# A gated-delta layer step: one TensorE transposition for two heads, decay factors scaled and first inverses made on GpSimd

## What is computed

```
kk = jnp.einsum('bnhid,bnhjd->bnhij', k, k)
a_mat = jnp.where(strict, beta[..., None] * kk * decay, 0.0) + jnp.eye(L, dtype=f32)
rhs = jnp.concatenate([v * beta[..., None], k * (beta * jnp.exp(gc))[..., None]], axis=-1)
sol = lax.linalg.triangular_solve(a_mat, rhs, left_side=True, lower=True, unit_diagonal=True)
...
qk = jnp.einsum('bnhid,bnhjd->bnhij', q, k) * decay
...
def step(s, inp):
    v_new = u_c - jnp.einsum('bhld,bhde->bhle', w_c, s)
    o = jnp.einsum('bhld,bhde->bhle', qd_c, s) + jnp.einsum('bhij,bhje->bhie', qk_c, v_new)
    s = s * gl_c[..., None, None] + jnp.einsum('bhld,bhle->bhde', kd_c, v_new)
```

## Time and profile before

| | us |
|---|---|
| median of 3 runs | 2017.8 |
| the profiled execution, its own time | 2012.97 |
| span of its trace | 2011.3 |
| group 0 of the delta stage, from its first pair products | 779.3 to 821.75 |
| group 1 | 821.75 to 862.05 |
| group 2 | 862.05 to 904.98 |
| group 3 | 904.98 to 945.69 |
| group 4 and its scan | 945.69 to 985.5 |

### The profile page before, as it was taken

The page is one execution under the profiler, slowest core; times in us unless marked ns, Lnnn a source line. Parts: engine busy times, 40 slices in busy tenths (PEclk is TensorE's granted clock), DMA queues, the critical chain, the costliest instruction groups (busy, mean ns, idle before and its releaser), DMA issues.

```text
span 2011.3 us, 34281 instructions
## 1 busy us (share of the span) xinstructions
PE 1936.1 (96%) x14050; PEld 1762.1 (88%) x14050; DVE 756.9 (38%) x1498; ACT 630.4 (31%) x1267; POOL 589.8 (29%) x456
## 2 busy tenths in 40 slices
PE   7999999999998998899799999999999999999998
PEld 7899999999995676678699879999999999999996
DVE  5211677111126764556643190222222222222225
ACT  5101222100016774344443244222222222222222
POOL 3111111111123003634264144333333333333333
PEclk9999999999999998999899999999999999999999
DMA  4322222622218213311253232111111111111114
GB/s 120 102 90 91 80 90 92 238 89 89 89 58 274 98 65 86 96 55 29 64 175 117 81 133 81 42 43 43 42 42 43 42 42 43 43 42 42 42 64 167
DMA packets 159274, 169.22 MB, mean 84 GB/s; under 512 B 14187, under 2 KB 130043, under 8 KB 159150
## 3 DMA queue, kind: packets, MB, share of 16 engines
q1 hardware_dynamic: 152814, 141.52, 22.6%
q10 hardware_dynamic: 6336, 25.96, 3.2%
HBM read 126.84 MB, written 40.55 MB: 83 GB/s over the span
## 4 chain that ended last, share of the span: by engine, by line
PE 49%; DVE 1%; ACT 0%; POOL 0%; issue 0%; DVEq 0%
PE t_B L2509 20%; PE t_B L2496 19%; PE t_B L2441 5%; PE t_B L2473 4%; DVE t_y L2356 1%; PE t_B L2451 0%; DVE t_y L2347 0%; DVE t_act_lo L2316 0%; ACT t_act_hi L2169 0%; DVE t_y L2386 0%; POOL t_wm_lo L2086 0%; ACT t_act_hi L2167 0%; DVE t_acc L2403 0%; DVE t_acc L2380 0%; DVE t_merged_lo L2363 0%
## 5 line engine op out<-in xcount | busy, mean ns | idle before, releaser
L2403 DVE TENSOR_TENSOR t_acc<-t_acc,t_B 128x512 f32<-128x512 f32 x252 | 173.3, 688 | 538.5 <-PE t_B L2509 538.5
L116 PE MATMUL i_ps<-x_hi,i_w_lo 128*128 128x384 f32 x1008 | 336.8, 334 | 0.0
L116 PE MATMUL i_ps<-x_hi,i_w_hi 128*128 128x384 f32 x1008 | 336.7, 334 | 0.0
L116 PE MATMUL i_ps<-x_lo,i_w_hi 128*128 128x384 f32 x1008 | 336.7, 334 | 0.0
L2496 PE MATMUL t_B<-t_merged_hi,t_wm_lo 128*128 128x384 f32 x768 | 256.9, 335 | 1.0 <-POOL t_wm_lo L2086 1.0
L2496 PE MATMUL t_B<-t_merged_lo,t_wm_hi 128*128 128x384 f32 x768 | 256.6, 334 | 0.0
L2496 PE MATMUL t_B<-t_merged_hi,t_wm_hi 128*128 128x384 f32 x768 | 256.6, 334 | 0.0
L106 POOL TENSOR_TENSOR i_w_lo<-i_w_raw,i_w_hi 128x1024 fp32r<-128x1024 f32 x44 | 105.7, 2403 | 432.2 <-ACT i_w_hi L101 432.2
L2086 POOL TENSOR_TENSOR t_wm_lo<-t_raw,t_wm_hi 128x1024 fp32r<-128x1024 f32 x49 | 119.0, 2428 | 295.9 <-ACT t_wm_hi L2161 295.9
L116 PEld LDWEIGHTS i_ps<-x_hi,i_w_lo 128*128 128x128 f32 x1008 | 189.2, 188 | 0.0
L116 PEld LDWEIGHTS i_ps<-x_lo,i_w_hi 128*128 128x128 f32 x1008 | 189.3, 188 | 0.0
(11 more groups left out here) (357 smaller groups left out, 3480.7 us busy)
## 6 DMA issues: line engine op xcount, KB each, us to landing
proj<-i_out ACTq DMA_DIRECT2D x44, 576.0 KB, 2.8
i_w_raw<-in_w_in SPq DMA_DIRECT2D x44, 512.0 KB, 3.7
t_raw<-in_w_up SPq DMA_DIRECT2D x32, 512.0 KB, 4.1
t_raw<-in_w_down SPq DMA_DIRECT2D x32, 512.0 KB, 3.5
t_gates<-proj SPq DMA_DIRECT2D x48, 192.0 KB, 2.6
a_k_cache<-in_cache_attn_k SPq DMA_DIRECT2D x8, 1024.0 KB, 8.0
a_v_cache<-in_cache_attn_v SPq DMA_DIRECT2D x8, 1024.0 KB, 5.4
d_c<-proj SPq DMA_DIRECT2D x3, 1536.0 KB, 7.6
```

The source lines that it names most:

```text
L116: last = pe.matmul(out, a[s][:, c, :], b[:, c, tokens], start=k == 0, stop=k == n - 1)
L2403: dve.tensor_tensor(a, a, B[(ND * j + d) % 4][:, :], ALU.add).then_inc(added, 1)
```

## The change

What it does:

- The channels of a group lie as [partition, chunk, channel block, token]. So two heads of one chunk are 128 adjacent columns, and "turn" takes four `pe.transpose` per chunk, each for two heads, where it took eight products. The loads now go chunk by chunk: 4 DMAs of 128 x 12 rows of 64 tokens (256 B), where one had rows of 256 tokens (1024 B), and `c0` takes 4 DMAs with such rows, where 2 had rows of 128 tokens (512 B).
- GpSimd multiplies `E` by `s_` for a whole group ("cols" has a part on GpSimd, one 128x512 operation), and "pair" on VectorE waits for that. `kd` takes `ers`, the product of `er` and `s_`.
- Step "x0" goes: its products on PE, two VectorE operations per chunk (1604), and `S0` on GpSimd (1412, step "turn"). In their place GpSimd makes `DD[1]` as identity minus the first masked block, in step "pair", after a wait for its own masking. "x0t" turns `DD[1]` into `DD[0]`.
- "sums" and "cols" of group g + 1 stand at other places: for g = 0 in steps "3a" and "3b", with the squares on ScalarE; else in "4b" and "5b". Before, "sums" stood after "solve", and "cols" after "pair" of the next group.
- `STEPS` keeps an empty step "turned" where "x0" stood, so scan items keep their step.

The diff's core (the rest gives waits and indices their new numbers and shapes; `head_c(n, c)` is the block c of chunk n, `landed(g)` is 16 for each load of the groups in this buffer up to g):

```diff
@@ -1117,10 +1117,10 @@
...
     def steps(n):
-        return (["pair", "turn", "x0", "x0t"] + [f"{j}{x}" for j in range(1, levels(n)) for x in "ab"]
+        return (["pair", "turn", "x0t"] + [f"{j}{x}" for j in range(1, levels(n)) for x in "ab"]
...

-    STEPS = ["pair", "turn", "x0", "x0t"] + [f"{j}{x}" for j in range(1, len(LEVELS)) for x in "ab"] + ["solve"]
+    STEPS = ["pair", "turn", "turned", "x0t"] + [f"{j}{x}" for j in range(1, len(LEVELS)) for x in "ab"] + ["solve"]
@@ -1150,14 +1150,14 @@
...
         if g:
-            out["pair"].insert(0, ("grp", g, "cols"))
...
             out["2b"].append(("grp", g + 1, "decay"))
-            out["solve"].append(("grp", g + 1, "sums"))
+            out["4b" if g else "3a"].insert(0, ("grp", g + 1, "sums"))
+            out["5b" if g else "3b"].append(("grp", g + 1, "cols"))
@@ -1178,9 +1178,9 @@
...
         if kind == "grp":
-            return {"decay": ("pool", "pe", "act"), "sums": ("pool" if n else "act", "pe", "dve"), "cols": ("pe", "act", "dve")}[s].count(eng)
+            return {"decay": ("pool", "pe", "act"), "sums": ("pool" if n > 1 else "act", "pe", "dve"), "cols": ("pe", "act", "dve", "pool")}[s].count(eng)
         if kind == "prep":
-            return {"pair": ("pe", "dve", "pool"), "turn": ("pe", "act", "dve", "pool"), "x0": ("pe", "dve"),
+            return {"pair": ("pe", "dve", "pool"), "turn": ("pe", "act", "dve"),
@@ -1314,10 +1319,10 @@
...
             def conv(g):
-                ts = first_token(GROUPS[g][0])
-                w = L * len(GROUPS[g])
-                sp.dma_start(C[g % 2][:, :, 0:w], env.proj[3 * AW:3 * AW + CONV, ts:ts + w].rearrange(
-                    "(c p) t -> p c t", p=P)).then_inc(c_in[g % 2], 16)
+                for n in GROUPS[g]:
+                    ts = first_token(n)
+                    sp.dma_start(C[g % 2][:, slot(n), :, :], env.proj[3 * AW:3 * AW + CONV, ts:ts + L].rearrange(
+                        "(c p) t -> p c t", p=P)).then_inc(c_in[g % 2], 16)
@@ -1361,12 +1366,20 @@
...
                 if kind == "grp" and s == "sums":
-                    w = L * len(GROUPS[n])
-                    pool.wait_ge(c_in[n % 2], 16 * ((n + 1) // 2))
+                    m = len(GROUPS[n])
+                    pool.wait_ge(c_in[n % 2], landed(n))
...
                     for i in range(2):
-                        half_c = C[n % 2][:, 4 * i:4 * i + 4, 0:w]
-                        pool.tensor_tensor(sq[i][:, :, 0:w], half_c, half_c, ALU.mult).then_inc(sq_made, 1)
+                        half_c = C[n % 2][:, 0:m, 4 * i:4 * i + 4, :].rearrange("p m h t -> p m (h t)")
+                        pool.tensor_tensor(sq[i][:, 0:m, :, :].rearrange("p m h t -> p m (h t)"), half_c, half_c,
+                                           ALU.mult).then_inc(sq_made, 1)
+                    continue
+                if kind == "grp" and s == "cols":
+                    m = GROUPS[n]
+                    wait(pool, "act", "grp", n, "decay")
+                    wait(pool, "dve", *item)
+                    e = E[n % 2][:, 0:len(m), :, :]
+                    did("pool", pool.tensor_tensor(e, e, bc(s_[:, m[0]:m[-1] + 1, :], 3, L), ALU.mult), item)
@@ -1392,7 +1405,12 @@
...
                     K = KQ[k][:, :, 1, :]
-                    ins = pool.tensor_tensor(M[k][:, 0:2, :, :], bc(K, 1, 2), bc(env.levc[:, 0:2, :], 2, 2), ALU.mult)
+                    pool.tensor_tensor(M[k][:, 0:2, :, :], bc(K, 1, 2), bc(env.levc[:, 0:2, :], 2, 2), ALU.mult
+                                       ).then_inc(first_blocks, 1)
+                    if n >= 4:
+                        wait(pool, "pe", "prep", solved(n - 4), "solve")
+                    pool.wait_ge(first_blocks, n + 1)
+                    ins = pool.tensor_tensor(DD[k][:, 1, :, :], bc(env.identc[:, :], 1, 2), M[k][:, 0, :, :], ALU.subtract)
@@ -1462,9 +1474,15 @@
...
                     elif s == "sums":
-                        act.wait_ge(env.c_in, 32)
+                        if n == 0:
+                            act.wait_ge(env.c_in, 64)
+                        else:
+                            act.wait_ge(c_in[1], landed(1))
+                            wait(act, "pe", "grp", 0, "sums")
                         for i in range(2):
-                            act.activation(sq[i][:, :, 0:w], C[0][:, 4 * i:4 * i + 4, 0:w], ACT.Square).then_inc(sq_made, 1)
+                            act.activation(sq[i][:, :, :, :].rearrange("p m h t -> p m (h t)"),
+                                           C[n][:, :, 4 * i:4 * i + 4, :].rearrange("p m h t -> p m (h t)"), ACT.Square
+                                           ).then_inc(sq_made, 1)
@@ -1573,12 +1591,14 @@
...
                         step(dve.tensor_tensor(s_[:, tiles, :], r2[:, tiles, :], beta[:, tiles, :], ALU.mult))
-                        ins = dve.tensor_scalar(negs[:, tiles, :], s_[:, tiles, :], -1.0, None, ALU.mult)
+                        if n == 0:
+                            dve.wait_ge(gexp, 3)
+                        ins = dve.tensor_tensor(ers[:, tiles, :], er[:, tiles, :], s_[:, tiles, :], ALU.mult)
...
                     if s == "pair":
-                        wait(dve, "act", "grp", n // 4, "decay")
+                        wait(dve, "pool", "grp", n // 4, "cols")
@@ -1589,26 +1609,15 @@
...
                             wait(dve, "pe", "heads", 3, "write")
-                        if n == 0:
-                            dve.wait_ge(gexp, 3)
...
                         dve.tensor_tensor(kbe[k][:, :, :], pairs(B[k][:, 0:256]), bc(eg[:, n, :], 2, P), ALU.mult)
-                        ins = dve.tensor_tensor(kd[n % 8][:, :, :], pairs(B[k][:, 0:256]), bc(er[:, n, :], 2, P), ALU.mult)
-                    elif s == "x0":
-                        wait(dve, "dve", "grp", n // 4, "cols")
-                        wait(dve, "pool", "prep", n, "turn")
-                        if n >= 4:
-                            wait(dve, "pe", "prep", n - 4, f"{last_level(n - 4)}a")
-                        for p in range(2):
-                            ins = dve.scalar_tensor_tensor(out=DD[k][:, 0, p, :], in0=B[k][:, p * L:p * L + L],
-                                                           scalar=negs[:, n, p:p + 1], in1=S0[k][:, p, :],
-                                                           op0=ALU.mult, op1=ALU.add)
+                        ins = dve.tensor_tensor(kd[n % 8][:, :, :], pairs(B[k][:, 0:256]), bc(ers[:, n, :], 2, P), ALU.mult)
...
                             wait(dve, "act", "prep", n, "x0t")
-                            wait(dve, "dve", "prep", n, "x0")
+                            wait(dve, "pool", "prep", n, "pair")
@@ -1726,32 +1735,27 @@
...
                         if n == 0:
-                            pe.wait_ge(env.c_in, 32)
+                            pe.wait_ge(env.c_in, 64)
                         elif n % 4 == 0:
-                            pe.wait_ge(c_in[n // 4 % 2], 16 * ((n // 4 + 1) // 2))
+                            pe.wait_ge(c_in[n // 4 % 2], landed(n // 4))
...
                             h = 2 * p + x
-                            ins = pe.matmul(b[half(x), 2 * L * p:2 * L * p + 2 * L], Cn[:, 4 + h, tok(n)], Cn[:, h:h + 5:4, tok(n)],
+                            ins = pe.matmul(b[half(x), 2 * L * p:2 * L * p + 2 * L], head_c(n, 4 + h), Cn[:, k, h:h + 5:4, :],
...
                         for i in range(2):
-                            for x, p in XP:
+                            for p in range(2):
                                 a = (2 * i + p) * P
-                                ins = pe.matmul(b[half(x), a:a + P], Cn[:, 4 + 4 * i + 2 * p + x, tok(n)], env.ident[:, :],
-                                                start=True, stop=True)
-                    elif s == "x0":
+                                ins = pe.transpose(b[:, a:a + P], Cn[:, k, 4 + 4 * i + 2 * p:6 + 4 * i + 2 * p, :].rearrange("p x t -> p (x t)"),
+                                                   env.ident[:, :])
+                    elif s == "x0t":
                         wait(pe, "dve", "prep", n, "turn")
-                        wait(pe, "pool", "prep", n, "turn")
+                        wait(pe, "pool", "prep", n, "pair")
                         for x, p in XP:
-                            ins = pe.matmul(b[half(x), p * L:p * L + L], M[k][half(x), 0, p, :], S0[k][half(x), p, :],
-                                            start=True, stop=True)
-                    elif s == "x0t":
-                        wait(pe, "dve", "prep", n, "x0")
-                        for x, p in XP:
-                            ins = pe.matmul(b[half(x), P + p * L:P + p * L + L], DD[k][half(x), 0, p, :],
+                            ins = pe.matmul(b[half(x), p * L:p * L + L], DD[k][half(x), 1, p, :],
...
```

37 lines of the change are left out of this document (17 added, 20 removed).

## The result

The changed kernel took 2035.7 us (median of 5 executions, 2031.5 to 2039.4), the kernel before 2018.8 beside it. The ratio is 1.0085, 95% interval 1.0068 to 1.0102: slower, by 17 us where +11.2 was predicted.

| part | before | after | difference | predicted |
|---|---|---|---|---|
| up to the first pair products | 779.31 | 785.38 | +6.1 | +0.5 |
| group 0 | 42.4 | 50.2 | +7.8 | +5.0 |
| group 1 | 40.3 | 44.1 | +3.8 | +1.7 |
| group 2 | 42.9 | 46.9 | +4.0 | +3.65 |
| group 3 | 40.7 | 44.1 | +3.4 | -0.2 |

A forecast was written before the change was run, and what follows sets the result against it. PE, nearly back to back, was taken to set the delta stage's pace, with group 0's mask chain lacking slack. Group terms of +9.15, attention +0.5 and clock +1.6 gave +11.2 on 2017.8: 2029.0 us, range 2014 to 2041.

The forecast's parts named there:

- Start of groups 2 and 3, -2.0: Heads of groups 2 and 3: second read and all behind it sooner with x0 gone, -2.0 us, bounds -1.3 and -2.25.
- Group 0, +5.0: Group 0: squares, table load and scaling ahead of the masks make them 6.9 us late; +5.0 us, bounds +3.5 and +6.5.
- Ends of groups 1 to 3, +1.7, +3.65, -0.2: Group ends: sums await squares and a load +3.0 us later, the norm follows, columns await Z7; net us per group.
- Short rows cost as much as those twice as long: Rival on the loads: 256 B rows cost 30 ns a packet like 512 B ones; 2037 us, chance 0.10.
- Group 4, -1.0: Last group, with two chunks: a sooner start makes it 1.0 us shorter.
- Attention, +0.5: c0's smaller packets ahead of the caches, while PE works on earlier blocks: +0.5 us, bounds 0 and 5.8.
- The clock, one fall, +1.6: PE's new waits at four places: one fall to 1.2 GHz counted in full, +1.6 us, bounds 0 and 6.4.
- The clock falls at all the heads: Rival: four clock falls at 1.6 us instead of one, perhaps because transpositions don't count as busy; 2033.8 us, chance 0.10.
- PE's stream decides: Rival on the delta stage: new waits fall into slack and the saved 12.4 us return in full; 2005.4 us, chance 0.14.

The follow-up runs named there:

- e2: The changed kernel with each chunk's four transpositions issued twice over into the same places: 2030.5 us, 1.0076 of the kernel before.
- e3: The changed kernel with x0t's products and copies one step earlier, ahead of the first out and second read: 2030.3 us, 1.0080 of the kernel before.
- e7: The changed kernel with c0's four transfers issued behind all the caches of attention: 2028.8 us, 1.0066 of the kernel before.
- e1: The changed kernel with each chunk turned by eight products with the identity, not four transpositions: 2036.8 us, 1.0091 of the kernel before.
- e4: The kernel before with only the new layout, loads with rows of 256 B and c0 in four transfers: 2018.1 us, ratio 1.0012.
- e5: The changed kernel with group 1's sums and columns back behind 4b and 5b: 2025.7 us, 1.0048 of the kernel before.
- e6: The changed kernel with the sums of groups 2 to 4 behind the norm, not ahead: 2029.8 us, 1.0057 of the kernel before.
- e9: e8 with c0's four transfers behind the caches of attention: 2007.5 us, 0.9964 of the kernel before.
- e12: e9 with idle products filling PE's waits ahead of group 0's first and second writes of the streams' states: 2009.3 us, 0.9957 of the kernel before.
- e8: The changed kernel's operations reordered (sums, columns, scaling, x0t moved; half the squares of groups 2 to 4 on ScalarE): 2011.3 us, 0.9973 of the kernel before.

## Why the prediction was right, and where its sizes were off

*Sign, main term and mechanism* were right: an order that puts new work ahead of the masks and the norm, and the squares on the path, costs more than the shorter stream gives. With the order mended, the same operations beat the kernel before.

*Start of groups 2 and 3, -2.0.* x0t came 9.7 us behind the pair products, 9.3 forecast and 11.5 before. The forecast gap of 2.9 us was 2.3; that gaps cost the clock as well stood in a rival.

*Group 0, +5.0.* The masks were 6.4 late (6.9 forecast); moving sums and columns back gave 7.5 us by the ratios and 9.2 in the profile. In e2 and e3 (clocks 0.88 and 0.89, against 0.81) the group was 5.4 to 5.9 longer than before, so the chain was sized well; the other 2 us in the profiled execution, which put it above the bound of +6.5, are most likely clock.

*Ends of groups 1 to 3, +1.7, +3.65, -0.2.* At a full clock group 1 took 40.5 (e7) and group 2 45.4 (e1, whose turn is longer), which is +0.2 and +2.5; group 3 took 40.2 at a full clock, though with e3's order, which is -0.5. So these terms were too high, by 1.5, 1.2 and 0.3 us. The price of 20 ns a packet was right, but I added all of the packets' growth to the load, and it was 1.6 us longer and not 3.0. The other mis-sized part is the norm: I took 1.7 to 2.0 us for it, and behind the squares it took 1.23, since 1.65 was its length beside them. In group 2 `turn0` thus came 36.2 us behind the pair products, against 34.9 before: +1.3 and not +3.0. "Short rows cost as much as those twice as long" is refuted in this case: 20.6 ns a packet of 256 B, 30 of 512. The Trainium skill (DMA: Bandwidth & Descriptors, Specifications) asks for at least 512 B a transfer for the full rate. The rate did fall, to 12.4 GB/s an engine from 17 at 512 B and 20 at 1024, by an estimate from these times; that a row of 256 B costs no less than one of 512, as the prediction read it, did not hold.

*Group 4, -1.0:* -1.3.

*Attention, +0.5: too low.* I reasoned that PE works on earlier blocks meanwhile. The rows show all caches behind c0 late, and the stage with them: 3.1 to 3.9 us more with four transfers than with two (under e7). The ratio of e4, +2.4 with 2.7 of uncertainty, agrees. It was inside my bounds, and the earlier trace rows pointed the other way: where the 16 engines are busy throughout, a longer transfer has no slack in which to hide. The other 2.7 us of the 6.1 in the table lie ahead of c0's issue and behind the stage's start, where profiles differ by as much whatever the kernel; the profile of the kernel before is itself 4.8 us faster than the median.

*The clock, one fall, +1.6: the step that failed in size.* 41 us at half speed instead of 7. The same code but for c0 (changed kernel and e7) had stages of 223.2 and 214.6 us at 41 and 17 us of low clock: 8.6 us for 24. By that the 34 us more than before are worth some 12 us in the profiled execution, in the medians less, since the profiles of the changed kernel and of e1, e2, e3, e5, e6 and e7 have 17 to 41, 27 on average: (27 - 7) x 0.36 = 7 us. The price of 0.36 comes from two profiles, but the lists of executions bear it out: in the four sets of the kernel before, 0.001 of mean clock, which is 4 us at the low level, went with 1.0 to 1.5 us, so 0.25 to 0.37 us each. I had said that "most of the lost time falls where PE then waits anyway"; the pair products of group 1 at 3.68 us in place of 1.97 (e9, e12) speak against it. "The clock falls at all the heads" was nearer to what happened than my forecast. Its named reason, the transposition, was wrong (e1, e2). What brings the falls is the order: with the same operations in e8's order the mean clock over all executions was 0.9880 and not 0.9806. That it does so through the waits is likely and rests on one execution of e12.

*"PE's stream decides":* refuted by e2, where 8 us of added work cost nothing.

So of +17 us in the medians, about 7.5 are the order in group 0 (its falls included), 3 to 4 c0, and about 1 the other groups apart from falls of the clock (+0.2, +2.5, -0.5, and -1.3 in group 4); the rest, some 5, is put down to those falls. That the order costs it is shown: e8 is 23 us faster with the same operations. The single shares are not measured that well; by the ratios each carries some 5 us, and only the profiles part them. That the sum of 11.2 lies as near to 17 as it does is in part luck: terms too high by 3 us at the ends of the groups made up for part of the clock and of c0.

## What to carry to other kernels

When a change makes an engine's stream shorter, look for what it waited with: here some 12 us of saved products turned into gaps, and several were followed by 3 to 10 us at half the clock. Before placing a new step in an in-order queue, write down what stands behind it on each of its engines; work that nobody awaits soon (here a scaling due 20 us later) belongs behind the chain, not ahead. A transfer placed ahead of others in a queue that is full delays all of them: c0, some 8 us of packets by an estimate (6208 at 20.6 ns on 16 engines), held the caches and the stage up by 4.8 us against c0 last. And when two instructions exclude each other, moving one beside the other gains nothing.

## What the runs showed of the hardware

- 6208 packets of 256 B took 20.6 ns each, against 30 for 512 B and 50 for 1024 B.
- A GpSimd product 128x1024 (1.89 us alone) and a VectorE product 128x1024 with both inputs in SBUF (1.23 alone) took turns: whichever began later ended about one own duration behind the other's end. VectorE took 2.60 us when it began 0.37 behind GpSimd (e8), GpSimd 2.87 when it began while VectorE waited or ran (e6).
- Stretches at 1.2 GHz of 3 to 10 us came behind waits of PE, but not behind each: in the changed kernel they follow waits of 1.64 (827.98) and 2.92 us (846.65) and even one of 0.97 (963.64), while in e7 waits of 2.35 (827.74) and 2.91 us (838.03) passed at the full clock. With the two of group 0 filled by products that nobody reads, none occurred between 790 and 970 in the one execution profiled, though single waits of 1.04 and 1.72 us were left in group 2. Between executions of nearly the same order the clock of group 1 was 0.91, 0.92 and 1.00 (changed kernel, e6, e7).
